# Gated linear attention's mix: from TensorE transposes to VectorE blocks sent through memory, with two roots in place of four

## The chip, the core and the metric

One core of a Trainium2 chip runs three transformer blocks as one program. The metric is device time in microseconds (us), the median of several runs. Engines by name: TensorE (PE, matmuls; PEld is its weight load), VectorE (DVE), ScalarE (ACT), GpSimd (POOL) and SyncE (SP), whose queue issues nearly all DMAs.

## The reference, cut to what matters

The change touches the end of the gated linear attention (four heads of 256 columns, 256 tokens) and the way its output reaches the product with `w_out`.

```python
    o = o_intra + o_inter.transpose(1, 2, 0, 3, 4)
    o = o.transpose(0, 2, 3, 1, 4).reshape(Bsz, S, H, DV)
    o = rms_norm(o, onorm_g)                                  # one root for each token and head
    o = o.reshape(Bsz, S, H * DV) * jax.nn.silu(r.astype(jnp.float32))
    ...
        mix = jnp.concatenate([out_a.astype(x.dtype), out_b.astype(x.dtype)], axis=-1)
        x = x + mix @ w_out[l]
```

`out_a` is this output, the first 1024 columns of the mix; `out_b` (the dilated attention) is the other half. A product contracts over the mix's columns, so they have to lie on the partitions: the mix must be transposed.

## The kernel before, in words

**The products.** Every weight matrix is streamed in units of 128 x 1024 numbers (two contraction tiles "kt" of 128 rows, 512 columns). A unit u is loaded into one of four buffers `raw` by SyncE (L2110, in order: the load of unit u + 4 is issued when VectorE is through with unit u), cut by ScalarE into a high part `wh` (L1347) and by VectorE into a low part `wl` (L1620); `wh` and `wl` have three buffers each, so the cut of unit u begins when unit u - 3 is multiplied. TensorE multiplies a unit in two halves of six matmuls (`mul`, L1154 to L1156: high by high, low by high, high by low), and the first half waits for the unit's `wl` and for the activations of its kts.

**The order of the work.** Every engine runs through one list, `plan.order`, and takes what is its own. `Plan` writes the list at build time in slots of 1.36 us (half a unit): lanes of generators say what comes when, and a `yield n` leaves n slots. What an engine finds in the list it does in that order; where it waits, all behind it on that engine waits.

**The stage around the change.** `w_out` has eight blocks of four units each (L56): first four blocks over kts 8 to 15 (the dilated half of the mix; units 101 to 116), then four over kts 0 to 7 (the gated half; units 117 to 132). While the first four run, `gla` (L534) makes the gated half: `g_o` (an output in PSUM for 128 tokens and two heads; ScalarE copies and squares it), `g_sum` (VectorE sums the squares), `g_root` (a reciprocal square root of 2 numbers per partition, 12 small VectorE instructions, L1601), `g_n` (two VectorE instructions: output times root times gate, into `va`), four times each. Then `mix` (L1166, L1357, L1632), four times, for two kts each: four TensorE transposes (L1088) into PSUM, two ScalarE instructions for the high part `mh`, two of VectorE for the low part `ml`. They stand between the halves of units 112 to 115. Unit 117 is the first to need kts 0 and 1, unit 118 kts 2 and 3, and so on.

**The way through memory**, which the kernel before uses for `x` and for nearly all mixes of the other attentions (`turned_and_sent` L416, `fetched` L430): `turn` (L1666) transposes blocks of 32 x 32 on VectorE into one of two places; `send` (L2152), four DMAs of SyncE, writes these to memory; `fetch` (L2161), one DMA, reads them back with the blocks in place; `xsent` or `msent` (L1370, L1654) cuts them into a high and a low part. Which place a turn takes alternates, and it waits until the send before the last one has landed:

```python
                    if n > 2:
                        on.wait_ge(*sent(plan.turns[n - 3]))
```

Of the kernel before, what the change touches and what calls it, by code (L numbers as in the profile page):

```python
# [152 lines left out]
class Plan:  # L153
# [276 lines left out]
    def fetched(self, p):  # L430

        yield 4
        while self.before[p] and self.before[p] not in self.said:
            yield 1
        self.say("fetch", *p)
        yield 6 if p[0] == "xsent" else 4
        self.say(*p)
# [96 lines left out]
    def gla(self):  # L534
        say = self.say
# [26 lines left out]
        for n in range(6):  # L562
            if n < 4:
                say("g_o", n)
            yield 1
            if 1 <= n < 5:
                say("g_sum", n - 1)
                say("g_root", n - 1)
            if n >= 2:
                say("g_n", n - 2)  # L570
            yield 1
        for h2 in range(2):
            for a in range(0, 4, 2):
                say("mix", "M0", 4 * h2 + a, "g", h2, a)
                yield 2

# [41 lines left out]
def program(nc, t, out):  # L618
# [76 lines left out]
    with ctx:  # L695
# [154 lines left out]
        decay = st[:, 400:416].rearrange("p (h c) -> p h c", h=4)  # L850
        rg = [st[:, 420 + 2 * m:422 + 2 * m] for m in range(4)]

        def w3(ap):
# [104 lines left out]
        def turn_places(p):  # L958

            n, (group, i) = (sents[p] - 1) % 2, plan.place[p]  # L960
            if group == "r":
                return PB[:, :, 256:384], A2[:, 5128:5640].rearrange("p (i n) -> p i n", i=4)
            first, then = {"d": (A2[:, 4096:5120], A2[:, 5120:6144]), "o": (A2[:, 2560:3584], A2[:, 3584:5632]),
                           "X1": (A2[:, 0:1024], A2[:, 4096:6144]), "X2": (A2[:, 0:1024], A2[:, 4096:6144]),
# [25 lines left out]
        def turn_place_free(p):  # L990

            kind = p[3] if p[0] == "msent" else p[1]
            if kind == "d":
                return [(s_move, moves[("move", "qk", "k", 1, 3)])]
            if kind == "X1":
                return [(s_pv, opened[("g_o", 3)]), (s_g_n, 4)]
# [41 lines left out]
        def turn_source(p):  # L1038

            if p[0] == "xsent":  # L1040
                return [x[:, k, 128 * p[2]:128 * p[2] + 256] for k in range(2)]
            return [AW[:, 512:1024] if p[3] == "o" else AW[:, 0:512]]

        def mix_source(p):

            if p[3] == "g":
                return lambda k, a: va[:, k, 512 * p[4] + 128 * (p[5] + a):512 * p[4] + 128 * (p[5] + a) + 128]
            return lambda k, a: AW[:, 512 + 256 * k + 128 * a:512 + 256 * k + 128 * a + 128]

        def turn_ready(p):  # L1050

            if p[0] == "xsent":
                return x_ready(int(p[1][1]), p[2] // 4)
            return {"d": (s_ob_dve, ob_n.get(("afin", "d", p[4]))), "r": (s_r_n, p[4] + 1), "o": (s_gated, p[4] + 1)}[p[3]]

        def gain_of(p):

            if p[0] in ("xturn", "xsent"):
                return [C(NORMS[int(p[1][1])], p[2] + i, p[2] + i + 1) for i in range(2)]
            return [C("on", 0, 1), C("on", 1, 2)] if p[3] == "g" else None  # L1060

# [20 lines left out]
        def tensor(e):  # L1082
# [8 lines left out]
            for p in plan.order:  # L1091
# [74 lines left out]
                elif kind == "mix":  # L1166
                    if p[3] == "g":
                        on.wait_ge(s_g_n, 2 * p[4] + 2)
                    else:
                        on.wait_ge(s_gated, nth("afin", "o", p[4]) - 4)  # L1170
                    on.wait_ge(*bank_free(*p))
# [412 lines left out]
        def vector(e):  # L1584
# [33 lines left out]
            for p in plan.order:  # L1618
# [307 lines left out]
                elif kind == "g_root":  # L1926
                    m = a[0]
                    root(rg[m], rg[m], 2, 256, (s_g_sum, m + 1))
                elif kind == "g_n":
                    m = a[0]  # L1930
                    k, h2 = gparts[m]
                    on.wait_ge(s_root, roots[("g_root", m)])
                    on.wait_ge(*taken(bi[("sr", 1)]))
# [330 lines left out]
```

## Time and profile before

| what | value |
|---|---|
| median of 3 runs | 1905.6 us (1905.49 to 1906.05) |
| the profiled execution, its own time | 1905.61 us |
| its span in the trace | 1903.7 us |
| TensorE busy | 1896.3 us (100%) |
| VectorE busy | 1268.9 us (67%) |
| ScalarE busy | 1001.3 us (53%) |
| DMA | 375.33 MB, mean 197 GB/s |

The span is the time from the first to the last instruction of the execution; the time beside it also has what lies around them, 1.9 us. Busy shares are over the whole span. Times inside the trace are counted from the start of the span.

### The profile page before, as it was taken

The numbers are of one execution on the slowest core, as the hardware profiler recorded it, in microseconds if no ns is written. First come the engines' busy times: TensorE is split into PE (matmuls) and PEld (weight loads), VectorE is DVE, ScalarE is ACT, GpSimd is POOL, SyncE is SP. The second block draws the span as 40 slices with busy tenths as digits, with TensorE's granted clock in tenths as the row PEclk, the third lists the DMA queues.
The fourth block names the chain that finished last, engine by engine and source line by source line (L and its number), as shares of the span: only waits on it lengthen the run. The fifth ranks groups of instructions, "written<-read, shape, count | busy, mean of one in ns | idle before, by whom it ended". The sixth has DMA issues, their size and how long they took to land.

```text
span 1903.7 us, 22784 instructions
## 1 busy us (share of the span) xinstructions
PE 1896.3 (100%) x8667; PEld 1561.9 (82%) x8667; DVE 1268.9 (67%) x1923; ACT 1001.3 (53%) x1409; POOL 14.4 (1%) x32
## 2 busy tenths in 40 slices
PE   9999999999999999999999999999999999999999
PEld 7888887888888888888888888888888888788887
DVE  6676566776666466665466776665766677777875
ACT  6777554454444344443444455654555554665653
POOL 0001000000000000000000000000000000000000
PEclk9999999999999999999999999999999999999999
DMA  9667754686666666666666786665676586555555
GB/s 323 201 189 183 208 178 133 203 256 195 195 190 196 192 188 194 196 195 197 191 194 192 219 268 194 193 194 174 195 210 195 192 263 213 165 167 165 154 169 166
DMA packets 211644, 375.33 MB, mean 197 GB/s; under 512 B 14592, under 2 KB 35376, under 8 KB 211536
## 3 DMA queue, kind: packets, MB, share of 16 engines
q1 hardware_dynamic: 210288, 371.12, 64.3%
q0 software_dynamic: 816, 2.11, 0.8%
q8 instruction: 68, 1.11, 0.2%
q10 hardware_dynamic: 432, 0.66, 0.1%
q14 instruction: 40, 0.33, 0.1%
HBM read 361.50 MB, written 12.33 MB: 196 GB/s over the span
## 4 chain that ended last, share of the span: by engine, by line
PE 98%; DVE 1%; ACT 0%; DMA 0%; issue 0%; SPq 0%; DVEq 0%; ACTq 0%
PE g L1154 31%; PE g L1156 31%; PE g L1155 31%; PE m L1223 1%; PE ob L1240 0%; PE ob L1241 0%; PE m L1088 0%; PE ob L1239 0%; DVE wl L1590 0%; PE m L1215 0%; PE m L1213 0%; DMA raw<-in_w_in 0%; PE m L1307 0%; PE ob L1294 0%; DVE st L1599 0%; PE ob L1288 0%
## 5 line engine op out<-in xcount | busy, mean ns | idle before, releaser
L1590 DVE TENSOR_TENSOR wl<-raw,wh 128x1024 fp32r<-128x1024 f32 (+1 forms) x660 | 802.6, 1217 | 559.3 <-ACT wh L1337 556.0
L1337 ACT ACTIVATE wh<-raw 128x1024 fp32r<-128x1024 f32 (+1 forms) x661 | 695.6, 1053 | 749.5 <-PE g L1156 742.1
L1154 PE MATMUL g<-wh,xh 128*128 128x512 f32 x1886 | 741.6, 393 | 0.6 <-DVE wl L1590 0.6
L1156 PE MATMUL g<-wh,xl 128*128 128x512 f32 x1886 | 735.1, 390 | 0.0
L1155 PE MATMUL g<-wl,xh 128*128 128x512 f32 x1886 | 734.5, 389 | 0.0
L1154 PEld LDWEIGHTS g<-wh,xh 128*128 128x128 f32 x1886 | 354.3, 188 | 78.7 <-issue 4.8
L1156 PEld LDWEIGHTS g<-wh,xl 128*128 128x128 f32 x1886 | 354.1, 188 | 74.4
L1155 PEld LDWEIGHTS g<-wl,xh 128*128 128x128 f32 x1886 | 354.4, 188 | 71.6
L1154 PE MATMUL g<-wh,mh 128*128 128x512 f32 x732 | 287.6, 393 | 0.0
L1156 PE MATMUL g<-wh,ml 128*128 128x512 f32 x732 | 285.2, 390 | 0.0
L1155 PE MATMUL g<-wl,mh 128*128 128x512 f32 x732 | 285.1, 390 | 0.0
L1154 PEld LDWEIGHTS g<-wh,mh 128*128 128x128 f32 x732 | 137.5, 188 | 31.6 <-issue 3.9
L1156 PEld LDWEIGHTS g<-wh,ml 128*128 128x128 f32 x732 | 137.5, 188 | 28.9
L1155 PEld LDWEIGHTS g<-wl,mh 128*128 128x128 f32 x732 | 137.5, 188 | 27.6
L1718 DVE STREAM_TRANSPOSE A<-A 32x256 f32<-32x256 f32 x176 | 76.7, 436 | 2.8
L1590 DVE TENSOR_TENSOR x<-g,x 128x512 f32<-128x512 f32 (+1 forms) x73 | 46.4, 676 | 12.1 <-PE g L1156 6.8
L1334 ACT ACTIVATE A<-g,st 128x512 f32<-128x512 f32 x50 | 31.6, 683 | 28.9 <-PE g L1156 28.9
L1337 ACT ACTIVATE A<-TW 32x256 f32<-32x256 f32 x96 | 39.9, 416 | 1.5
L1337 ACT ACTIVATE mh<-A 128x256 fp32r<-128x256 f32 (+1 forms) x56 | 26.9, 506 | 23.8 <-DVE A L1718 16.4
L1590 DVE TENSOR_TENSOR ml<-A,mh 128x256 fp32r<-128x256 f32 (+1 forms) x56 | 29.0, 540 | 13.9 <-ACT mh L1337 13.9
L1337 ACT ACTIVATE PT<-m 128x384 f32<-128x384 f32 x40 | 18.2, 489 | 37.5 <-PE m L1223 37.5
L1593 DVE SCALAR_TENSOR_TENSOR xl<-A,small,xh 128x128 fp32r<-128x128 f32 (+1 forms) x112 | 34.0, 362 | 5.4 <-ACT xh L1337 5.4
(154 smaller groups left out, 818.5 us busy)
## 6 DMA issues: line engine op xcount, KB each, us to landing
raw<-in_ev_w_in SPq DMA_DIRECT2D x128, 512.0 KB, 3.8
raw<-in_w_in SPq DMA_DIRECT2D x92, 512.0 KB, 4.3
raw<-in_w_gate SPq DMA_DIRECT2D x88, 512.0 KB, 4.4
raw<-in_w_up SPq DMA_DIRECT2D x88, 512.0 KB, 4.3
raw<-in_w_down SPq DMA_DIRECT2D x88, 512.0 KB, 4.8
raw<-in_od_w_in SPq DMA_DIRECT2D x72, 512.0 KB, 4.2
raw<-in_w_out SPq DMA_DIRECT2D x32, 512.0 KB, 4.7
raw<-in_ev_w_out SPq DMA_DIRECT2D x32, 512.0 KB, 4.8
```

Of the source, the lines that this page charges most:

```text
L1154: e.matmul(o, hi[:, kt, c], h, start=first, stop=False)
L1155: e.matmul(o, hi[:, kt, c], l, start=False, stop=False)
L1156: last = e.matmul(o, lo[:, kt, c], h, start=False, stop=end)
L1223: last = e.transpose(o[:, 128 * c:128 * c + 128], L[:, 128 * c:128 * c + 128], ident)
L1334: return e.activation(o, i, func, scale=scale, bias=bias)
L1337: return e.activation(o, i, AF.Copy, scale=scale)
L1590: return e.tensor_tensor(o, a, b, op)
L1593: return e.scalar_tensor_tensor(out=o, in0=a, scalar=s, in1=b, op0=op0, op1=op1)
L1718: last = e.transpose(dst, src)
```

## The change

The gated half of the mix takes the way through memory. `mix` for kind "g" goes; in its place stand four times `turn` (two VectorE transposes of 128 x 256 from `va`), `send`, `fetch` and `msent` (two ScalarE instructions, four of VectorE, since the norm's weight is a scale). The four roots of 2 numbers become two of 4 (one for each pair of heads), and `g_n` 0 and 1 stand behind the first, 2 and 3 behind the second.

```diff
--- before.py
+++ after.py
@@ -433,7 +433,7 @@
         while self.before[p] and self.before[p] not in self.said:
             yield 1
         self.say("fetch", *p)
-        yield 6 if p[0] == "xsent" else 4
+        yield 6 if p[0] == "xsent" or p[3] == "g" else 4
         self.say(*p)
 
     def moved_by_blocks(self, key, j):
@@ -562,17 +562,23 @@
         for n in range(6):
             if n < 4:
                 say("g_o", n)
+            else:
+                say("g_n", n - 3)
             yield 1
             if 1 <= n < 5:
                 say("g_sum", n - 1)
-                say("g_root", n - 1)
-            if n >= 2:
-                say("g_n", n - 2)
+            if n in (2, 4):
+                say("g_root", n // 2 - 1)
+            if n == 4:
+                yield from self.turned_and_sent("msent", "M0", 0, "g", 0, 0)
+            if n in (3, 5):
+                say("g_n", n - 3 if n == 3 else 3)
             yield 1
-        for h2 in range(2):
-            for a in range(0, 4, 2):
-                say("mix", "M0", 4 * h2 + a, "g", h2, a)
-                yield 2
+            if n == 4:
+                yield from self.turned_and_sent("msent", "M0", 2, "g", 0, 2)
+        for a in range(0, 4, 2):
+            yield from self.turned_and_sent("msent", "M0", 4 + a, "g", 1, a)
+            yield 1
 
     def retention(self):
         say = self.say
@@ -849,6 +855,7 @@
         nsink = st[:, 352:384]
         decay = st[:, 400:416].rearrange("p (h c) -> p h c", h=4)
         rg = [st[:, 420 + 2 * m:422 + 2 * m] for m in range(4)]
+        rg2 = [st[:, 420 + 4 * h2:424 + 4 * h2] for h2 in range(2)]
 
         def w3(ap):
             return ap.rearrange("p (t n) -> p t n", t=2)
@@ -960,7 +967,7 @@
             n, (group, i) = (sents[p] - 1) % 2, plan.place[p]
             if group == "r":
                 return PB[:, :, 256:384], A2[:, 5128:5640].rearrange("p (i n) -> p i n", i=4)
-            first, then = {"d": (A2[:, 4096:5120], A2[:, 5120:6144]), "o": (A2[:, 2560:3584], A2[:, 3584:5632]),
+            first, then = {"d": (A2[:, 4096:5120], A2[:, 5120:6144]), "g": (A2[:, 0:1024], A1[:, 1024:3072]), "o": (A2[:, 2560:3584], A2[:, 3584:5632]),
                            "X1": (A2[:, 0:1024], A2[:, 4096:6144]), "X2": (A2[:, 0:1024], A2[:, 4096:6144]),
                            "X3": (A1[:, 0:1024], A1[:, 1024:3072])}[group]
             a, b = first[:, 512 * n:512 * n + 512], then[:, 512 * i:512 * i + 512]
@@ -992,6 +999,8 @@
             kind = p[3] if p[0] == "msent" else p[1]
             if kind == "d":
                 return [(s_move, moves[("move", "qk", "k", 1, 3)])]
+            if kind == "g":
+                return [(s_pv, opened[("g_o", 3)])]
             if kind == "X1":
                 return [(s_pv, opened[("g_o", 3)]), (s_g_n, 4)]
             if kind == "r":
@@ -1039,25 +1048,26 @@
 
             if p[0] == "xsent":
                 return [x[:, k, 128 * p[2]:128 * p[2] + 256] for k in range(2)]
+            if p[3] == "g":
+                return [va[:, k, 128 * p[2]:128 * p[2] + 256] for k in range(2)]
             return [AW[:, 512:1024] if p[3] == "o" else AW[:, 0:512]]
 
         def mix_source(p):
 
-            if p[3] == "g":
-                return lambda k, a: va[:, k, 512 * p[4] + 128 * (p[5] + a):512 * p[4] + 128 * (p[5] + a) + 128]
             return lambda k, a: AW[:, 512 + 256 * k + 128 * a:512 + 256 * k + 128 * a + 128]
 
         def turn_ready(p):
 
             if p[0] == "xsent":
                 return x_ready(int(p[1][1]), p[2] // 4)
-            return {"d": (s_ob_dve, ob_n.get(("afin", "d", p[4]))), "r": (s_r_n, p[4] + 1), "o": (s_gated, p[4] + 1)}[p[3]]
+            return {"d": (s_ob_dve, ob_n.get(("afin", "d", p[4]))), "g": (s_g_n, 2 * p[4] + 2), "r": (s_r_n, p[4] + 1),
+                    "o": (s_gated, p[4] + 1)}[p[3]]
 
         def gain_of(p):
 
             if p[0] in ("xturn", "xsent"):
                 return [C(NORMS[int(p[1][1])], p[2] + i, p[2] + i + 1) for i in range(2)]
-            return [C("on", 0, 1), C("on", 1, 2)] if p[3] == "g" else None
+            return [C("on", 0, 1), C("on", 1, 2)] if p[0] == "msent" and p[3] == "g" else None
 
         def aw_free(*p):
 
@@ -1164,10 +1174,7 @@
                     four(lambda c: v[:, c // 2, 128 * (c % 2):128 * (c % 2) + 128],
                          lambda c: x[:, c % 2, 128 * (kt + c // 2):128 * (kt + c // 2) + 128]).then_inc(s_bank, 1)
                 elif kind == "mix":
-                    if p[3] == "g":
-                        on.wait_ge(s_g_n, 2 * p[4] + 2)
-                    else:
-                        on.wait_ge(s_gated, nth("afin", "o", p[4]) - 4)
+                    on.wait_ge(s_gated, nth("afin", "o", p[4]) - 4)
                     on.wait_ge(*bank_free(*p))
                     v = bank(*p)[:, :].rearrange("p (k t) -> p k t", k=2)
                     src = mix_source(p)
@@ -1924,12 +1931,12 @@
                     reduce(rg[m], (Z if m % 2 == 0 else K)[:, 512:1024].rearrange("p (g d) -> p g d", d=256),
                            ALU.add).then_inc(s_g_sum, 1)
                 elif kind == "g_root":
-                    m = a[0]
-                    root(rg[m], rg[m], 2, 256, (s_g_sum, m + 1))
+                    h2 = a[0]
+                    root(rg2[h2], rg2[h2], 4, 256, (s_g_sum, 2 * h2 + 2))
                 elif kind == "g_n":
                     m = a[0]
                     k, h2 = gparts[m]
-                    on.wait_ge(s_root, roots[("g_root", m)])
+                    on.wait_ge(s_root, roots[("g_root", h2)])
                     on.wait_ge(*taken(bi[("sr", 1)]))
                     on.wait_ge(s_pv, opened[("g_o", min(m + 2, 3))])
                     on.wait_ge(*moved("g_state", 2, h2))
```

TensorE's list loses four groups of transposes like the one here, and nothing else. Before, between the halves of unit 112:

```order
L1154 MATMUL g<-wh,mh 128x512
L1155 MATMUL g<-wl,mh 128x512
L1156 MATMUL g<-wh,ml 128x512
L1088 MATMUL m<-small,A 128x128 [waits s_g_n]
L1088 MATMUL m<-small,A 128x128 x3
L1154 MATMUL g<-wh,mh 128x512
L1155 MATMUL g<-wl,mh 128x512
```

Each group is four transposes (here the two rows of L1088); the matmuls around them stand in the same order in both lists.

VectorE's list before, from the last root on. `A<-A,st` is `g_n` 2 and 3, `wl<-raw,wh` the cuts of units 113, 114 and 115, `ml<-m` a mix, `x<-g,x` the adding of block 15:

```order
L1593 SCALAR_TENSOR_TENSOR st<-st 128x2 [waits s_dve_step]
L1593 SCALAR_TENSOR_TENSOR A<-A,st 128x256 [waits s_bank_dve,s_root]
L1593 SCALAR_TENSOR_TENSOR A<-A,st 128x256
L1590 TENSOR_TENSOR wl<-raw,wh 128x1024 [waits s_hi]
L1593 SCALAR_TENSOR_TENSOR A<-A,st 128x256 [waits s_root]
L1593 SCALAR_TENSOR_TENSOR A<-A,st 128x256
L1590 TENSOR_TENSOR wl<-raw,wh 128x1024 [waits s_hi]
L1593 SCALAR_TENSOR_TENSOR ml<-m,small,mh 128x256 [waits s_split]
L1593 SCALAR_TENSOR_TENSOR ml<-m,small,mh 128x256
L1590 TENSOR_TENSOR x<-g,x 128x512 [waits s_mul]
L1590 TENSOR_TENSOR x<-g,x 128x512
L1590 TENSOR_TENSOR wl<-raw,wh 128x1024 [waits s_hi]
```

VectorE's list of the change at the same place; the first turn and the cut of unit 113 stand just ahead of it. `A<-A 128x2x4x32` is a turn (two instructions each), `A<-A,st` is `g_n` 2 and 3, and the cuts are those of unit 114 and, first of the last row, 115:

```order
L1683 STREAM_TRANSPOSE A<-A 128x2x4x32 [waits s_send1]
L1683 STREAM_TRANSPOSE A<-A 128x2x4x32
L1600 SCALAR_TENSOR_TENSOR A<-A,st 128x256 [waits s_bank_dve,s_root]
L1600 SCALAR_TENSOR_TENSOR A<-A,st 128x256 x3
L1597 TENSOR_TENSOR wl<-raw,wh 128x1024 [waits s_hi]
L1683 STREAM_TRANSPOSE A<-A 128x2x4x32 [waits s_send0,s_g_n]
L1683 STREAM_TRANSPOSE A<-A 128x2x4x32
L1683 STREAM_TRANSPOSE A<-A 128x2x4x32 [waits s_send1]
L1683 STREAM_TRANSPOSE A<-A 128x2x4x32
L1597 TENSOR_TENSOR x<-g,x 128x512 [waits s_mul]
L1597 TENSOR_TENSOR x<-g,x 128x512
L1597 TENSOR_TENSOR wl<-raw,wh 128x1024 [waits s_hi] x3
```

The cut of unit 115 stands behind all four turns now; the third waits for the first send (`s_send0`), the fourth for the second (`s_send1`).

SyncE's list of the change. `raw<-in_w_out` is a load of weights (units 117, 118 and 119), `blocks<-A` a send (four DMAs), `A<-blocks` a fetch:

```order
L2166 DMA blocks<-A 32x4x128 [waits s_fetch0,s_turn]
L2166 DMA blocks<-A 32x4x128 x3
L1090 DMA raw<-in_w_out 128x2x512 [waits s_lo]
L2166 DMA blocks<-A 32x4x128 [waits s_fetch1,s_turn]
L2166 DMA blocks<-A 32x4x128 x3
L1090 DMA raw<-in_w_out 128x2x512 [waits s_lo]
L2166 DMA blocks<-A 32x4x128 [waits s_fetch2,s_turn]
L2166 DMA blocks<-A 32x4x128 x3
L2166 DMA blocks<-A 32x4x128 [waits s_fetch3,s_turn]
L2166 DMA blocks<-A 32x4x128 x3
L2173 DMA A<-blocks 128x512 [waits s_send0]
L1090 DMA raw<-in_w_out 128x2x512 [waits s_lo]
```

Before, nothing but loads stood here; now the first fetch is behind all four sends.

## Rows read from the trace of the kernel before

**Rows 1.** The page: busy time, granted TensorE clock in 40 slices, chain that ended last.
```profile
PE 1896.3 (100%) x8667; PEld 1561.9 (82%) x8667; DVE 1268.9 (67%) x1923; ACT 1001.3 (53%) x1409; POOL 14.4 (1%) x32
...
PEclk9999999999999999999999999999999999999999
...
PE 98%; DVE 1%; ACT 0%; DMA 0%; issue 0%; SPq 0%; DVEq 0%; ACTq 0%
```
**Rows 2.** Source line 1088 between 300 and 600 us: duration ns min/median/max, first and last start.
```profile
L1088 PE MATMUL m<-small,A x16: 270/272/273, 338.2 to 348.1; 128*128 128x128 f32 x16
```
**Rows 3.** Timeline of PE: start us, us, engine, line, operation, out<-in, count.
```profile
338.16 0.60 PE L1088 MATMUL m<-small,A 128*128 128x128 f32 x4
...
341.35 0.60 PE L1088 MATMUL m<-small,A 128*128 128x128 f32 x4
...
346.36 0.39 PE L1154 MATMUL g<-wh,mh 128*128 128x512 f32 x1
...
352.28 0.39 PE L1154 MATMUL g<-wh,mh 128*128 128x512 f32 x1
...
355.00 0.39 PE L1154 MATMUL g<-wh,mh 128*128 128x512 f32 x1
```
**Rows 4.** Timeline of DVE, 324 to 345 us; in brackets the idle time before.
```profile
324.16 0.17 DVE L1606 TENSOR_SCALAR st<-st 128x2 f32<-128x2 f32 x1
...
334.56 0.68 DVE L1599 TENSOR_REDUCE st<-A 128x2 f32<-128x512 f32 x1
335.28 0.17 DVE L1606 TENSOR_SCALAR st<-st 128x2 f32<-128x2 f32 x1
...
337.55 0.88 DVE L1593 SCALAR_TENSOR_TENSOR A<-A,st 128x256 f32<-128x256 f32 x2
338.34 1.22 DVE L1590 TENSOR_TENSOR wl<-raw,wh 128x1024 fp32r<-128x1024 f32 x1
339.48 0.88 DVE L1593 SCALAR_TENSOR_TENSOR A<-A,st 128x256 f32<-128x256 f32 x2
340.27 1.22 DVE L1590 TENSOR_TENSOR wl<-raw,wh 128x1024 fp32r<-128x1024 f32 x1
...
342.19 1.28 DVE L1590 TENSOR_TENSOR x<-g,x 128x512 f32<-128x512 f32 x2
343.38 1.22 DVE L1590 TENSOR_TENSOR wl<-raw,wh 128x1024 fp32r<-128x1024 f32 x1
```
**Rows 5.** Timeline of ACT.
```profile
331.62 1.06 ACT L1337 ACTIVATE wh<-raw 128x1024 fp32r<-128x1024 f32 x1 [0.37 <-PE g L1156]
...
377.99 0.89 ACT L1337 ACTIVATE xh<-A,small 128x256 fp32r<-128x256 f32 x2
```
**Rows 6.** Timeline of DVE, where x is turned and fetched in the same way.
```profile
365.69 0.76 DVE L1676 STREAM_TRANSPOSE A<-x 128x256 f32<-128x256 f32 x2
...
390.13 0.76 DVE L1676 STREAM_TRANSPOSE A<-x 128x256 f32<-128x256 f32 x2
390.82 1.09 DVE L1593 SCALAR_TENSOR_TENSOR xl<-A,small,xh 128x128 fp32r<-128x128 f32 x4
```
**Rows 7.** Timeline of SPq (SyncE's queue of DMA issues), 366 to 385 us.
```profile
366.49 1.83 SPq L2159 DMA_DIRECT2D blocks<-A  x4
368.48 0.39 SPq L1080 DMA_DIRECT2D raw<-in_w_out  x1
...
372.21 0.34 SPq L2166 DMA_DIRECT2D A<-blocks  x1
...
377.37 1.80 SPq L2159 DMA_DIRECT2D blocks<-A  x4
...
384.23 0.34 SPq L2166 DMA_DIRECT2D A<-blocks  x1
```
**Rows 8.** Source line 2159 (sends), 200 to 420 us: issue to landing.
```profile
DMA to landing us min/median/max: 2.1/3.5/5.5
```
**Rows 9.** Source line 2166 (fetches), the same stretch.
```profile
DMA to landing us min/median/max: 4.2/4.9/6.0
```

## The prediction

> **What bounds the kernel now.** I read the page first. TensorE is busy all the time, the chain that ended last is 98% TensorE, and its clock stands at full speed in every slice [rows 1]. So a microsecond of TensorE's list taken away is a microsecond won, and a wait of TensorE is one lost, wherever it falls. VectorE's 67% is a mean and settles nothing. I then read the stage of the gated mix from the timelines of TensorE, VectorE, ScalarE and SyncE. Between 334 and 344 us VectorE goes from one instruction to the next without idle time [rows 4]. The last question is how long a send and a fetch take; no gated mix goes that way yet, but x does 30 us later [rows 6 to 9].
>
> **What is removed.** Sixteen transposes [rows 2], in four groups. The first group begins at 338.16 and the second at 341.35, with two halves of a unit (12 matmuls in all) between them: 3.19 us. The same two halves without a group take 355.00 - 352.28 = 2.72 us [rows 3]. A group therefore costs TensorE 0.47 us, and the four cost **1.88 us**. That is all the change can win; two roots of 2.27 us (335.28 to 337.55, [rows 4]) go from VectorE too, but VectorE's time counts only where TensorE waits for it.
>
> The Trainium skill speaks against the change ("VectorE: DVE Perf Modes", The three transpose paths, and its rules for kernel authors): a full 128 x 128 transpose belongs on TensorE where a PSUM destination will do, since VectorE turns only blocks of 32 x 32. Its table gives 390 ns for one on TensorE, an estimated 6.2 us for sixteen; by that the case below in which TensorE waits for nothing would end at 1899.4 instead of 1903.7, and the sum, which ends in a wait, would stay. The row's 0.47 us for four does not agree with it, and is used.
>
> **What is added on VectorE, and where.** I build a ladder from the rows, start to start: cut of a unit 1.14 (338.34 to 339.48), `g_n` 0.79, adding a block 1.19, `g_sum` 0.72, root 2.27 [rows 4]; turn 0.69 [rows 6]. A root of 4 numbers is taken at the price of one of 2: these are tiny instructions in a dependent chain. The first root begins at 324.16 as before, and what stands ahead of the cut of unit 112 (root, block 14, cut 111, `g_sum` 2, `g_n` 0) is through at about 330.5. That cut cannot start earlier, because ScalarE's part starts at 331.62 and takes 1.06 [rows 5]. So: cut 112 at 332.7, `g_n` 1 at 333.85, `g_sum` 3 at 334.65, second root 335.35, first turn 337.6, cut 113 at 338.3, second turn 339.45, `g_n` 2 and 3 at 340.15 and 340.95, cut 114 at 341.75, and VectorE is free for the third turn at 342.9. The work saved in roots has been lost in the wait for cut 112: cut 113 stands where it stood (338.34).
>
> **The new wait.** The third turn waits until the first send has landed, the fourth until the second has, and behind them in VectorE's list stand block 15 and the cut of unit 115. A send is issued 0.80 us after its turn starts (365.69, 366.49) and takes 1.99 us of SyncE's queue (to 368.48). The first one of x was issued at 366.49, and the fetch that waits for it went at 372.21: 5.7 us [rows 6, 7]. Another took 6.9 (377.37 to 384.23). The single DMAs of sends take 2.1 to 5.5 us from issue to landing, 3.5 in the middle [rows 8], and the last of four is issued 1.4 us after the first: bounds of 3.5 and 6.9 us for a send. I take 5.7, the send that like these has one load of weights just ahead of it.
>
> The first send is then issued at 338.4 and has landed at 344.1; a load of weights follows, the second send goes at 340.9 and has landed at 346.6. Third turn 344.1, fourth 346.6, block 15 at 347.3, cut 115 at 348.5, ready (1.22 us long) at 349.7, TensorE goes on at 349.8.
>
> TensorE began unit 115 at 346.36 [rows 3]; with three groups of transposes gone it would be there at 344.95. It idles **4.85 us**. Cut 113 (ready 339.55) and cut 114 (ready 343.0) are a little late as well, 0.1 and 0.6 us; that is part of the 4.85, not on top.
>
> **The first fetch.** Unit 117 needs kts 0 and 1. From the start of unit 115 it was 352.28 - 346.36 = 5.92 us away, now 5.45: 355.25. In SyncE's list the first fetch stands behind all four sends: third send 344.9 to 346.9, fourth 347.4 to 349.4, fetch at 349.4. Fetches land after 4.2 to 6.0 us, 4.9 in the middle [rows 9]: 354.3. ScalarE's part takes 0.89 [rows 5], VectorE's 1.09 [rows 6], TensorE goes on at 356.4: **1.15 us** more. With the fetch at 4.2 it is 0.45, at 6.0 it is 2.25.
>
> After that nothing is late by this ladder. The third mix, needed by unit 119 at 361.85, is ready at 361.9. Loads of weights are issued up to 3 us later behind the sends; that of unit 119 (349.9) would be there at 354.8 if it takes as long as a fetch, and ScalarE wants it at 357. Costed at nothing: ScalarE's four pairs of instructions (as many as before), 2 MB more DMA traffic on 375 MB, VectorE's two more instructions for each mix (in time that it has while TensorE multiplies), and the later stages, whose lists are the same and which only start later. Their cover is VectorE's and ScalarE's waiting for TensorE.
>
> **Sum.** -1.88 + 4.85 + 1.15 = +4.1 us on the profiled execution's own 1905.61, which is also the median of the three runs: **1909.7 us**. The same comes out directly: unit 117 begins at 356.4 instead of 352.28, and all behind it moves with it. From no change a measurement tells about 0.2%, 3.8 us; the forecast lies just beyond.
>
> **Rivals.**
>
> *Quick sends.* For it speaks that SyncE's loads stand back here: the first send finds little else in flight, and the middle DMA of a send takes 3.5 us, so a send 4.9. Then the fourth turn starts at 345.8, cut 115 is ready at 348.9, TensorE idles 4.05, and with a fetch of 4.2 only 0.45 later on: +2.6, 1908.2 us. At the bound of 3.5 us it idles 2.65 and then 0.95, because now four sends in a row in SyncE's queue hold the fetch: +1.7, 1907.3 us. Against it speak both sends that a fetch waited for, 5.7 and 6.9. The Trainium skill ("DMA: Bandwidth & Descriptors", Anatomy of one DMA) gives a fixed 2 us, most of it the write's receipt, plus the bytes at 436 GB/s. For 64 KB that is an estimated 2.15 us, a send of 3.5 and 1907.3 us here; the rows' 3.5 us for a single DMA, under a stream of weights, do not agree with it.
>
> *Slow sends.* 6.9 us for a send and 6.0 for a fetch: TensorE goes on with unit 115 at 351.0 (6.05 idle), and waits 2.25 for the first mix: +6.4, 1912.0 us.
>
> *The clock falls.* TensorE never stops for microseconds in the trace of before, and its clock is full in all slices [rows 1]; here it stops for 4 us in one piece. If it came back at 1.2 GHz, each half of a unit (1.36 us) would take as much again: for the four halves up to unit 117 5.4 us, of which the 1.15 of waiting are hidden, 1914.0 us; for two of them 1911.2. The Trainium skill ("TensorE: Matmul & The Clock Gate", What's actually happening) says that the slow clock is the default and that an idle engine falls back to it. Nothing in the trace of before shows a fall.
>
> *Not slower.* VectorE gets the cut of unit 115 ready before TensorE wants it, at 344.9, and the 1.88 us stand alone: 1903.7 us. It decides whether that cut starts by 343.65. Even without any wait for a landing the ladder has it at 342.9 + two turns + block 15 = 345.45 and ready at 346.65, so VectorE would have to be 1.8 us faster than its rows, and the first fetch as much earlier.
>
> **How the numbers follow.** Forecast 0.50 (its own range 1908.9 to 1910.8), quick sends 0.27, slow sends 0.13, clock 0.05, not slower 0.05. Slower by over 0.2% (above 1909.4): some two thirds of the forecast's case, the slow sends and the clock: 0.52. Within 0.2%: the rest of the forecast, the quick sends and nearly all of the last case (-1.9 us is within it as well): 0.46. Faster: 0.02. The range goes from 1907.0 (just under the quick sends' bound) to 1912.6 (just over the slow ones).
>
> **What would show it.** No L1088 transposes into mh's banks between 338 and 348 us; VectorE's turns start at about 337.6, 339.5, 344.1 and 346.6, the last two with idle time ahead that a DMA into memory ended; TensorE idle for some 4 us before unit 115, released by the low part of the weights, and about 1 us before unit 117, released by the low part of the mix. TensorE's other rows are unchanged. The prediction is wrong if the fourth turn starts before 344, if TensorE idles elsewhere (a load of weights late behind the sends), or if the clock's row shows less than 9.

## The result, and the profile after

The change takes **1908.65 us** (median of 20 runs, 1907.59 to 1909.64); the kernel before, on the same chip, 1905.45 (20 runs, 1905.24 to 1906.08). The ratio is 1.0016, with a 95% interval of 1.001 to 1.0022: 3.2 us slower. The profiled execution of the change took 1909.28 us (span 1907.5), against 1905.61 (span 1903.7) before: 3.67 us more.

The page of the change, where [rows 1] stood: busy time, granted TensorE clock in 40 slices, and the chain that ended last.

```profile
PE 1897.8 (99%) x8651; PEld 1561.1 (82%) x8651; DVE 1268.9 (67%) x1915; ACT 1001.0 (52%) x1409; POOL 14.4 (1%) x32
...
PEclk9999999999999999999999999999999999999999
...
PE 97%; DVE 2%; ACT 0%; SPq 0%; DMA 0%; issue 0%; DVEq 0%; ACTq 0%
```

TensorE has 16 instructions less, as the diff says, and yet 1.5 us more of busy time: some of the rest became slower. The chain now goes through VectorE for 2% of the span, where 1% stood (both are rounded). The clock's row shows nothing; its slices are 48 us long.

The list of waits of the change (engine and line that waited, what for: us in total, times, longest) has one wait of TensorE for a low part of the weights that is longer than 2 us, and one turn that waited for a send:

```profile
PE g L1164 <- DVE wl L1597: 2.9, 2, 2.5
...
DVE A L1683 <- DMA blocks<-A: 1.8, 1, 1.8
```

VectorE's timeline of the change (start, duration, then engine, line, operation, out<-in, count; in brackets the idle time before and what ended it), against [rows 4]:

```profile
332.85 1.23 DVE L1597 TENSOR_TENSOR wl<-raw,wh 128x1024 fp32r<-128x1024 f32 x1 [2.32 <-ACT wh L1344]
...
337.76 0.77 DVE L1683 STREAM_TRANSPOSE A<-A 128x256 f32<-128x256 f32 x2
338.45 1.18 DVE L1597 TENSOR_TENSOR wl<-raw,wh 128x1024 fp32r<-128x1024 f32 x1
...
341.79 1.22 DVE L1597 TENSOR_TENSOR wl<-raw,wh 128x1024 fp32r<-128x1024 f32 x1
342.93 0.77 DVE L1683 STREAM_TRANSPOSE A<-A 128x256 f32<-128x256 f32 x2
345.49 0.77 DVE L1683 STREAM_TRANSPOSE A<-A 128x256 f32<-128x256 f32 x2 [1.79 <-DMA blocks<-A]
346.18 1.25 DVE L1597 TENSOR_TENSOR x<-g,x 128x512 f32<-128x512 f32 x2
347.36 3.47 DVE L1597 TENSOR_TENSOR wl<-raw,wh 128x1024 fp32r<-128x1024 f32 x3
```

The cut of unit 112 (332.85) still waits for ScalarE, so the shorter roots bring nothing; from there to the cut of unit 114 the predicted ladder holds to within 0.2 us. Then comes the fourth turn, which waits 1.79 us for the second send. The third turn did not wait. Behind the fourth stand block 15 and the cut of unit 115 (347.36, before 343.38).

TensorE's timeline of the change, against [rows 3]:

```profile
345.69 0.39 PE L1166 MATMUL g<-wh,ml 128*128 128x512 f32 x1
348.61 0.53 PE L1164 MATMUL g<-wh,mh 128*128 128x512 f32 x1 [2.54 <-DVE wl L1597]
348.95 0.62 PE L1165 MATMUL g<-wl,mh 128*128 128x512 f32 x1
...
351.93 0.60 PE L1166 MATMUL g<-wh,ml 128*128 128x512 f32 x1
352.36 0.41 PE L1164 MATMUL g<-wh,mh 128*128 128x512 f32 x1
...
355.80 0.39 PE L1164 MATMUL g<-wh,mh 128*128 128x512 f32 x1
```

The last matmul of unit 114 starts at 345.69 and unit 115 begins at 348.61. After that stop the matmuls do not come every 0.23 us but every 0.42, up to 352.36. Unit 117 (355.80) finds its activations ready; nothing holds it. The table by stretch (busy time and instructions of each engine, then the granted clock, the DMA share and GB/s) shows what the 40 slices hide:

```profile
340.00:349.00 9.00, 6.11 (x26) 4.39 (x25) 7.21 (x14) 3.10 (x3) 0.00 (x0) 1.00 0.82 222
349.00:352.50 3.50, 3.50 (x10) 2.73 (x9) 2.45 (x5) 0.91 (x2) 0.00 (x0) 0.52 0.91 233
352.50:360.00 7.50, 7.50 (x35) 6.18 (x34) 6.10 (x15) 5.60 (x9) 0.00 (x0) 1.00 0.87 314
```

The granted clock was 0.52 for 3.5 us, that is, nearly all of it at the lower level of 1.2 GHz, after a stop of 2.54 us. It did not fall during the stop: read in shorter stretches it is 1.00 from 345.5 to 348.6 and 0.50 only from 349.0 on, when TensorE has been at work again for 0.4 us. Of the 20 runs 12 have a mean clock of 0.999 and a median of 1908.8 us; the other 8 have 1.000 and a median of 1907.88. So the fall comes in some runs and not in others, with the same program. The mean clock is a coarse sign of it: it has three digits, and a fall to half for under some 1.9 us (an estimate: half of that is 0.0005 of 1907 us) would still read 1.000. Five of the 8 took 1907.6 to 1908.0 us, the other three 1908.3 to 1908.6, and those may hide a short one.

SyncE's queue in the change, against [rows 7]; `blocks<-A` is a send, `A<-blocks` a fetch:

```profile
338.56 1.78 SPq L2166 DMA_DIRECT2D blocks<-A  x4
340.38 0.45 SPq L1090 DMA_DIRECT2D raw<-in_w_out  x1
340.93 1.88 SPq L2166 DMA_DIRECT2D blocks<-A  x4
...
343.72 4.29 SPq L2166 DMA_DIRECT2D blocks<-A  x8
348.06 0.44 SPq L2173 DMA_DIRECT2D A<-blocks  x1
```

The trace's answers from issue to landing (minimum, median, maximum), against [rows 8, 9]: the first send, the second send, and the four fetches of the change.

```profile
DMA to landing us min/median/max: 1.7/1.8/1.8
...
DMA to landing us min/median/max: 3.0/3.1/3.3
...
DMA to landing us min/median/max: 2.8/5.7/6.4
```

The second send, issued at 340.93, had landed when the fourth turn began at 345.49: 4.56 us. The first was issued at 338.56 and cannot have taken more than 4.37, since the third turn began at 342.93 without a wait; its last DMA was issued at 339.9 and none took more than 1.8, so it took about 3.1. The first fetch landed in 2.8 us: ScalarE began its mix at 350.87, the low part was ready at 353.0, and TensorE came to it only at 355.80.

**The sum as measured.** All earlier work of this trace lies 0.14 us later than before (the cut of unit 112 by ScalarE begins at 331.76 instead of 331.62). Without three groups of transposes unit 115 would begin at 346.36 - 1.41 + 0.14 = 345.09; it begins at 348.61: 3.52. From there to unit 117 it is 7.19 us instead of 5.45: 1.74, nearly all of it for the clock. (Some 0.14 of it is the start after a stop: in the last kernel below, after a stop of 0.74 us and with a clock of 1.00, two halves of a unit take 2.86 us instead of 2.72.) So -1.88 + 3.52 + 1.74 = +3.38, and with the 0.14 the 3.52 by which unit 117 is later than before, of 3.67 in all.

### The profile page after: what moved, and what is told of

It is laid out like the page before. It is cut to its first block, busy times and chain, and to the rows that moved or that the text cites. A ratio compares the mean times of both kernels' runs of the same rounds, so it can differ in the third digit from the quotient of the medians.

```text
span 1907.5 us, 22773 instructions
## 1 busy us (share of the span) xinstructions
PE 1897.8 (99%) x8651; PEld 1561.1 (82%) x8651; DVE 1268.9 (67%) x1915; ACT 1001.0 (52%) x1409; POOL 14.4 (1%) x32
## 4 chain that ended last, share of the span: by engine, by line
PE 97%; DVE 2%; ACT 0%; SPq 0%; DMA 0%; issue 0%; DVEq 0%; ACTq 0%
PE g L1164 31%; PE g L1166 31%; PE g L1165 31%; PE m L1230 1%; DVE wl L1597 0%; PE ob L1247 0%; PE ob L1248 0%; PE ob L1246 0%; PE m L1098 0%; PE m L1222 0%; PE m L1220 0%; PE m L1314 0%; DVE st L1606 0%; PE ob L1301 0%; PE ob L1295 0%; PE m L1106 0%
```

## The experiments

Eight kernels were run, each 11 times beside the kernel before on the same chip. What is called "the theory" in the expectations is: the transposes are worth 1.9 us, the staging places make VectorE late for the cut of unit 115, and the clock falls after that stop.

### What the transposes cost: twice as many

The kernel before, with the sixteen transposes made twice:

```diff
-                    four(lambda c: v[:, c // 2, 128 * (c % 2):128 * (c % 2) + 128],
-                         lambda c: src(c % 2, c // 2)).then_inc(s_bank, 1)
+                    for i in range(2 if p[3] == "g" else 1):
+                        last = four(lambda c: v[:, c // 2, 128 * (c % 2):128 * (c % 2) + 128],
+                                    lambda c: src(c % 2, c // 2))
+                    last.then_inc(s_bank, 1)
```

> The kernel before, with each of the sixteen transposes of the gated mix made twice by TensorE into the same place. It measures by itself what the change takes away. Theory (0.47 us for a group, of which some 0.12 is the switch between shapes, which is not doubled): 4 x 0.35 to 0.47 = 1.4 to 1.9 us more than before, 1906.9 to 1907.4. Rival (a transpose costs what it lasts, 0.27 us, or the weights' way is the limit): 16 x 0.27 = 4.3 us, 1909.8.

It took 1907.46 us (1907.24 to 1908.47), the kernel before 1905.55; ratio 1.0011, interval 1.0002 to 1.002. TensorE's timeline of this kernel:

```profile
338.11 1.03 PE L1088 MATMUL m<-small,A 128*128 128x128 f32 x8
...
341.74 1.03 PE L1088 MATMUL m<-small,A 128*128 128x128 f32 x8
```

From group to group it is 3.63 us, with groups of four 3.19 [rows 3]. A doubled group costs 0.44 more, four of them 1.76, and the median rose by 1.9. The interval is wide for so small a difference, but all 11 runs lie above all 33 of the kernel before (1905.19 to 1906.03). That agrees with the 1.88 us, and with TensorE's list being paid for one to one here.

The Trainium skill ("VectorE: DVE Perf Modes", The three transpose paths) gives 390 ns for a 128 x 128 transpose on TensorE, in a table for bf16, while these are fp32; by that the doubling would have cost an estimated 6.2 us. The runs do not agree: one more transpose in a row costs 0.11 us.

### The wait for the staging place: a place for each turn

The change, with a place of their own for the third and fourth turn and four semaphores for the sends, so that no turn has to wait for a landing:

```diff
+            if group == "g" and i >= 2:
+                first = A1[:, 5120:6144]
...
-            return s_send[n % 2], 64 * (n // 2 + 1)
+            return s_send[n % 4], 64 * (n // 4 + 1)
...
-                    if n > 2:
+                    if n > 2 and not (a[0] == "msent" and a[3] == "g" and plan.place[a][1] >= 2):
                         on.wait_ge(*sent(plan.turns[n - 3]))
```

> The third and fourth turn of the change get staging places and send semaphores of their own, so that no turn waits for a landing; the order of every engine stays. Theory (the fourth turn's wait for the second send, 1.79 us, is what makes the cut of unit 115 late, and the stop it makes is long enough to bring the slow clock): fourth turn at 343.6 right behind the third, cut 115 at about 345.6, TensorE goes on at about 346.9 instead of 348.6, idle about 1.8 us before unit 115; no fall of the clock, so 1907.6 - 1.75 = 1905.9 us in every run, beside 1905.45 of before. First rival (the landings cost nothing; VectorE's work or the loads of weights are late by themselves): 1907.6 to 1908.7 as the change. Second rival (the first fetch behind four sends takes over): TensorE waits before unit 117 for up to 1 us, 1906.9.

It took 1907.7 us (1907.13 to 1908.19), beside 1905.55; ratio 1.0011, interval 1.0003 to 1.002. That was missed: about 1 us better than the change, and 1.8 us worse than expected. Even this 1 us can be the clock alone: the change's own runs with a mean clock of 1.000 have a median of 1907.88. VectorE's timeline shows that the edit does what it should:

```profile
342.68 1.42 DVE L1685 STREAM_TRANSPOSE A<-A 128x256 f32<-128x256 f32 x4
...
345.19 2.34 DVE L1599 TENSOR_TENSOR wl<-raw,wh 128x1024 fp32r<-128x1024 f32 x2
```

Four transposes stand in a row with no idle time, and the cut of unit 115 begins at 345.19 instead of 347.36. TensorE's timeline shows where the gain went, at the starts of units 115, 117, 118 and 119:

```profile
346.45 0.50 PE L1166 MATMUL g<-wh,mh 128*128 128x512 f32 x1 [0.62 <-DVE wl L1599]
...
352.84 0.47 PE L1166 MATMUL g<-wh,mh 128*128 128x512 f32 x1 [0.65 <-issue]
...
356.23 0.47 PE L1166 MATMUL g<-wh,mh 128*128 128x512 f32 x1 [0.38 <-DVE ml L1602]
...
359.61 0.47 PE L1166 MATMUL g<-wh,mh 128*128 128x512 f32 x1 [0.40 <-DVE ml L1602]
```

From unit 115 to 117 it is 6.39 us instead of 5.45, and then twice some 3.38 instead of 2.72: 2.27 us of waiting for the mixes. Unit 119 begins 1.89 us later than before (357.72 there), and the whole execution was 1.93 longer. The fetches are the cause. This is the answer of the trace for the four of them:

```profile
DMA to landing us min/median/max: 3.3/6.2/6.8
```

They are issued from 347.27 on, less than 1 us earlier than in the change, because all four sends still stand ahead of them in SyncE's list. ScalarE waits for the first one, and VectorE for ScalarE, in their timelines:

```profile
350.58 0.91 ACT L1346 ACTIVATE mh<-A,small 128x256 fp32r<-128x256 f32 x2 [3.60 <-DMA A<-blocks]
...
351.60 1.14 DVE L1602 SCALAR_TENSOR_TENSOR ml<-A,small,mh 128x128 fp32r<-128x128 f32 x4 [2.93 <-ACT mh L1346]
```

The low part is through at 352.74 and unit 117 begins at 352.84, though the record of that matmul calls its wait "issue". TensorE arrives 2.2 us earlier than in the change and finds nothing ready. So two chains end nearly together here: the staging place's, and send, issue queue and fetch. To take away the first uncovers the second, as the second rival of the expectation had it, but for three units and not for one. No stop between 322 and 372 us is longer than 0.65 us by the records, and the mean clock is 1.000 in all runs.

### The fall of the clock: fill the stop

The change, with fourteen matmuls that nobody reads, ahead of unit 115:

```diff
+                    if u == 115 and half == 0:
+                        for i in range(14):
+                            e.matmul(MB[0][:, :], mh[:, 8, 0:128], mh[:, 8:10, :], start=True, stop=True)
```

> The change, with 14 matmuls more on TensorE just before unit 115 into a PSUM bank that nobody reads, so that TensorE works through most of the time in which it waits for the cut of unit 115 (14 x 0.23 = 3.2 us of 3.5). Theory (the stop lets the clock fall, and this is what splits the 20 runs of the change into 1907.6 to 1908.0 with a mean clock of 1.000 and around 1908.7 with 0.999): all runs at a mean clock of 1.000 and 1907.6 to 1907.9 us, 1 us less than the change's median although TensorE does more, and matmul starts 0.23 us apart after unit 115 begins. Rival (the 1 us comes from transfers that land later in some runs, and the clock only goes with it): two groups of runs as before, median 1908.7.

It took 1907.57 us (1907.32 to 1909.05), beside 1905.55; ratio 1.0012, interval 1.0003 to 1.0021. TensorE's timeline of this kernel:

```profile
345.59 3.34 PE L1143 MATMUL m<-mh 128*128 128x512 f32 x14
348.77 0.39 PE L1167 MATMUL g<-wh,mh 128*128 128x512 f32 x1
349.00 0.40 PE L1168 MATMUL g<-wl,mh 128*128 128x512 f32 x1
...
360.28 0.47 PE L1167 MATMUL g<-wh,mh 128*128 128x512 f32 x1 [0.40 <-DVE ml L1603]
```

The row of its table by stretch that answers to the slow one of the change:

```profile
349.00:352.50 3.50, 3.50 (x17) 2.90 (x16) 2.41 (x5) 1.61 (x3) 0.00 (x0) 1.00 0.88 227
```

TensorE is as late for unit 115 as in the change (348.77), but it was at work, and the clock stays at 1.00: matmuls every 0.23 us, 17 of them in a stretch in which the change got 10 done. The fall is therefore a consequence of the stop, and more work makes the kernel 1.1 us faster (1908.65 for the change, and 1908.7 for its twin of the next experiment, which ran beside this one on the same chip). It is less than the 1.74 us that the clock took in the trace: at full clock TensorE comes to unit 119 before its mix, and waits 0.55 us from start to start (359.50 + 0.23 to 360.28). Slow matmuls had covered that. Eight of the 11 runs took 1907.3 to 1907.7, three 1908.2 to 1909.05, all with a mean clock of 1.000. A varying lateness of the fetches would fit, but only one of these executions (1908.18) has a trace, so what sets the three apart stays open.

### The number of roots, in the change

The change with four roots of 2 numbers, as before (the planner is also told that a root costs half, so that the order of the rest stays):

```diff
-            if n in (2, 4):
-                say("g_root", n // 2 - 1)
+                say("g_root", n - 1)
...
-                    h2 = a[0]
-                    root(rg2[h2], rg2[h2], 4, 256, (s_g_sum, 2 * h2 + 2))
+                    m = a[0]
+                    root(rg[m], rg[m], 2, 256, (s_g_sum, m + 1))
```

> The change with four roots of 2 numbers again, one behind each sum, and the planner told that they cost half, so that all else stands nearly where the change has it (two turns of x one unit earlier). Theory (two roots in place of four won nothing, because VectorE waits 2.32 us before the cut of unit 112 in the change and has room for one of them, and the other stands where the joint root stood): cut 113 at 338.3 to 338.5, the time equal to the change, 1907.6 or 1908.7 as the clock goes. Rival (each root on VectorE's path counts 2.27 us): turns 2 to 4.5 us later, TensorE waits as much longer before unit 115, 1910.5 to 1912.

It took 1908.7 us (1907.9 to 1909.09), beside 1905.55; ratio 1.0016, interval 1.0007 to 1.0025. That is the time of the change. VectorE's timeline of this kernel:

```profile
338.31 1.18 DVE L1596 TENSOR_TENSOR wl<-raw,wh 128x1024 fp32r<-128x1024 f32 x1
...
345.31 0.77 DVE L1682 STREAM_TRANSPOSE A<-A 128x256 f32<-128x256 f32 x2 [1.76 <-DMA blocks<-A]
```

TensorE's:

```profile
348.44 0.50 PE L1163 MATMUL g<-wh,mh 128*128 128x512 f32 x1 [2.51 <-DVE wl L1596]
```

The cut of unit 113, the wait and the stop are those of the change, to 0.2 us. The two roots saved fall into the 2.32 us in which VectorE waits for ScalarE's part of unit 112.

### The two roots alone

The kernel before with two roots of 4 numbers, and the mix on TensorE as it was:

```diff
-                say("g_root", n - 1)
-            if n >= 2:
-                say("g_n", n - 2)
+            if n in (2, 4):
+                say("g_root", n // 2 - 1)
+            if n >= 3:
+                say("g_n", n - 3)
+            if n == 5:
+                say("g_n", 3)
```

> The kernel before with two roots of 4 numbers in place of four, the mix still turned by TensorE: the half of the change that leaves TensorE's list alone. Theory (TensorE waits for nothing in this stage before, so VectorE's saved time wins nothing): 1905.5 us, no difference, VectorE idle some 2.3 us more before the cut of unit 112. Rival (the shorter chain lets the mix and all behind it come earlier): 1903 to 1905.

It took 1905.37 us (1905.14 to 1906.22), beside 1905.6; ratio 0.9999, interval 0.999 to 1.0008. Nothing, as expected. In VectorE's timeline of this kernel

```profile
337.43 1.22 DVE L1593 TENSOR_TENSOR wl<-raw,wh 128x1024 fp32r<-128x1024 f32 x1
```

is the cut of unit 113, 0.9 us earlier than in [rows 4], and TensorE does not ask for it earlier.

### The third and fourth turn behind the cuts

The change, with block 15 and the cut of unit 115 ahead of the third turn, and the cut of unit 116 ahead of the fourth:

```diff
+        yield 2
         for a in range(0, 4, 2):
             yield from self.turned_and_sent("msent", "M0", 4 + a, "g", 1, a)
-            yield 1
+            yield 2
```

> The change with its third turn behind block 15 and the cut of unit 115, and its fourth behind the cut of unit 116: the order alone, with two staging places as in the change. Theory (the stop before unit 115 is a matter of what stands behind the waiting turn): TensorE goes on with unit 115 without a stop of more than 0.2 us, the clock never falls; but the third and fourth mix come 3 us later than in the change, and TensorE waits before unit 119 for 1.4 to 3 us: 1906 to 1907.5. Rival (the time goes to the transfers whatever the order): 1907.6 or more.

It took 1908.84 us (1907.23 to 1910.1), beside 1905.6; ratio 1.0015, interval 1.0006 to 1.0024. Missed: that is in the range of the rival. There is no stop ahead of unit 115 any more, but TensorE's timeline shows such a stop 11 us later, ahead of unit 119:

```profile
359.74 0.47 PE L1165 MATMUL g<-wh,mh 128*128 128x512 f32 x1 [2.63 <-DVE ml L1601]
...
361.36 0.63 PE L1167 MATMUL g<-wh,ml 128*128 128x512 f32 x1
```

SyncE's timeline has the third fetch,

```profile
351.30 0.52 SPq L2174 DMA_DIRECT2D A<-blocks  x1
```

and ScalarE's the instructions that wait for it:

```profile
357.45 0.91 ACT L1345 ACTIVATE mh<-A,small 128x256 fp32r<-128x256 f32 x2 [2.33 <-DMA A<-blocks]
```

It is issued at 351.30 and has landed by 357.45, 6.15 us later; TensorE stopped for 2.63 us, and the clock fell again (0.63 us a matmul, in 6 of the 11 runs by their mean clock). The turns can be early, and delay a cut, or late, and delay a mix.

### The turns in VectorE's idle time

The change, with `g_n` 0 and 1 and the first two turns ahead of the cut of unit 112, where VectorE has been waiting for ScalarE in every kernel so far:

```diff
-            if n == 4:
+            if n == 3:
+                say("g_n", 0)
+                say("g_n", 1)
                 yield from self.turned_and_sent("msent", "M0", 0, "g", 0, 0)
...
+                yield from self.turned_and_sent("msent", "M0", 2, "g", 0, 2)
             yield 1
...
+            if n >= 4:
+                say("g_n", n - 2)
```

> The change with another order: g_n 0 and 1 and the first two turns and sends stand ahead of the cut of unit 112, in the 2.32 us in which VectorE waited for ScalarE; the second root, g_n 2 and 3 and the last two turns move up behind them. Theory (the way through memory is worth its 1.88 us once no turn finds a send under way and the first fetch isn't behind four sends): first turn at about 331.1, first fetch at about 338.6, third and fourth turn at 340.7 and 341.4 without a wait, cut 115 at 343.3, TensorE never stops between 325 and 360 us, 1905.5 - 1.9 = 1903.6 to 1903.7 us, faster than both kernels. Rival (as the run with places of its own showed, when one stop goes the next limit comes up: the fetches of kts 4 to 7 are issued with loads of weights and land after 6 us): TensorE waits before unit 119, 0.4 us or more, 1904.0 to 1904.6. Second rival (loads of weights are late behind early sends): stops at units 116 or 117, 1905 or more.

It took **1903.72 us** (1903.45 to 1904.54), beside 1905.6; ratio 0.999, interval 0.9981 to 0.9999. It beats both kernels: the kernel before by 1.88 us, what the transposes cost. The interval nearly reaches 1, but all 11 runs lie below all 33 of the kernel before (1905.34 to 1906.45). VectorE's timeline:

```profile
331.20 1.42 DVE L1682 STREAM_TRANSPOSE A<-A 128x256 f32<-128x256 f32 x4
332.69 1.23 DVE L1596 TENSOR_TENSOR wl<-raw,wh 128x1024 fp32r<-128x1024 f32 x1
...
340.79 1.43 DVE L1682 STREAM_TRANSPOSE A<-A 128x256 f32<-128x256 f32 x4
...
343.31 2.34 DVE L1596 TENSOR_TENSOR wl<-raw,wh 128x1024 fp32r<-128x1024 f32 x2
```

The third and fourth turn come 9 us after the first two, when the places are long free, and the cut of unit 115 begins at 343.31, just before the 343.65 that the rival "not slower" asked for. The first two fetches go at 338.50, nearly ten us before those of the change, so that the 4.3 to 7.0 us that fetches take here are hidden. TensorE has no idle time between 330 and 370 us.

### The same with four roots

The order of the kernel just above with four roots of 2 numbers (its edit and that of "The number of roots, in the change" together).

> The early order with four roots of 2 numbers in place of two of 4, all else of the plan the same. Theory (in this order VectorE has no wait left that would hide a root, so the two roots count): cut 113 late by 0.5 us and cut 115 at about 345.3, 2 us later than with two roots; TensorE stops about 0.7 and 1.0 us, 1903.65 + 1.7 = 1905.3 us. Rival (the roots don't matter in any order, as in the change): the time of the early order.

It took 1905.64 us (1905.3 to 1906.07), beside 1905.6; ratio 1.0, interval 0.9991 to 1.0009. Now TensorE stops twice for the low part of the weights, as its timeline shows:

```profile
340.43 0.50 PE L1162 MATMUL g<-wh,mh 128*128 128x512 f32 x1 [0.73 <-DVE wl L1595]
...
346.91 0.50 PE L1162 MATMUL g<-wh,mh 128*128 128x512 f32 x1 [0.74 <-DVE wl L1595]
```

In this order VectorE has nothing left over, and the two roots saved are worth 1.9 us. (The unit after this second stop begins at 349.77; the granted clock is 1.00 there.) The same edit was worth nothing in the kernel before and nothing in the change.

## Why the prediction was right, point by point

The forecast was 1909.7 us and the measurement 1908.65: 4.1 us slower forecast, 3.2 found. The direction, the place and the wait were right; two terms of the sum were too large, and one that stood among the rivals took part of their room. The time lies below the forecast's own narrow range (from 1908.9) and within the 0.2% for which the prediction had the smaller chance (0.46, against 0.52 for more).

1. **Transposes, -1.88.** Right: 0.44 for each doubled group, 1.9 us in the median.
2. **Roots are worth nothing.** Right, shown twice, by four roots in the change and by two roots alone.
3. **The ladder up to the cut of unit 114.** Right to 0.2 us: first turn 337.76 (337.6), cut of unit 113 338.45 (338.3), cut of unit 114 341.79 (341.75).
4. **Idle time ahead of unit 115, 4.85.** Right in kind, too large: 3.52, of which 2.54 is one stop; most of the rest was lost at unit 114, as the ladder had it. The term that was mis-sized is the 5.7 us for a send. It came from a send of x with other traffic about. Here the first send took about 3.1, below the lower bound of 3.5, and the second 4.56, so the third turn waited for nothing and the fourth began at 345.49 instead of 346.6. The rival "quick sends" (4.9 us a send, idle 4.05, 1908.2 us) was nearer to this than the forecast, in the wait and in the time.
5. **First fetch, 1.15.** Wrong in the change: TensorE did not wait for it at all. The fetch was issued at 348.06, 1.3 us earlier than in the ladder, and it landed in 2.8 us, below all of [rows 9]. The mix was through at 353.02, so that TensorE would not have waited without the slow matmuls either (355.80 less 1.74). But the fetches are the next to be late: they cost 2.27 us as soon as the first wait is taken away, and 0.55 in the trace where the stop is filled.
6. **The clock.** This had a chance of 0.05, and it came in 12 of 20 runs. The price was also too high: two or four halves at half speed were reckoned, and it was one and a third, some 1.6 us in the trace (1.74 with the start after the stop) and 1.1 between the medians of the change and of the kernel with the stop filled. The Trainium skill ("TensorE: Matmul & The Clock Gate", What's actually happening) says that an idle engine falls back to the lower clock; the trace agrees, 0.52 after the stop and 1.00 where the stop was filled. To hold "no fall is seen in the trace of before" against it was weak: once TensorE is under way, no wait of it in that trace is longer than 1.1 us. And the sign that the prediction named, a clock row below 9, could not show it: the row reads 9 throughout, and the clock fell.

The sum of the forecast (-1.88 + 4.85 + 1.15 = +4.1) and that of the trace (-1.88 + 3.52 + 1.74 = +3.4) are near each other in part by luck: the stop and the fetch came out 2.5 us smaller than forecast (1.33 and 1.15), and the clock, which the sum had at nothing, put 1.74 back. Without the clock the change would have taken 1907.9 by its own eight runs with a mean clock of 1.000, and 1907.6 by the kernel with the stop filled; the forecast was 1.8 to 2.1 us above that.

## What to carry to other kernels

Taking work off the engine that sets the time pays only as long as what replaces it finds idle time on the others, so put it where an engine waits anyway: the same turns cost 3.2 us behind the cut of unit 112 and won 1.9 us ahead of it. With two chains that end nearly together (a staging place that must be free, a fetch behind four sends in one queue), take one away and the other shows; give both their lead at once, by issuing earlier. Cost a stop of some 2.5 us by its idle time plus, in part of the runs, a stretch at half clock, and read the clock in a table of short stretches, since slices of 48 us hide it.

## What the runs showed of the hardware that was not expected

- **One stop, then half speed.** After TensorE stood for 2.54 us in the middle of a program that had run at full clock, the granted clock was 0.52 for 3.5 us. It began to fall only after the engine was back at work: in the change 0.3 to 0.4 us after, with late turns 0.8 us (restart at 359.74 after 2.63 us, first slow matmul at 360.52). By the mean clock of each run it came in 12 of 20 runs of the change, 9 of 11 with four roots and 6 of 11 with late turns. Stops of 0.4 to 0.7 us were followed by no fall. What decides between two runs of the same program was not found.
- **Filler work can win.** Fourteen useless matmuls in the stop made the program 1.1 us faster.
- **Landing times went with their company.** In the change a DMA of the first send landed in 1.8 us, one of the second, with a load of weights just ahead in SyncE's queue, in 3.1; of four fetches the first, right behind the sends, took 2.8 us, and the others, issued after one or two more loads, 5.3, 6.2 and 6.4. No run changes the company alone, so this cause is not shown. The Trainium skill ("DMA: Bandwidth & Descriptors", Anatomy of one DMA) gives, for DMAs that GpSimd issues, a fixed 2 us plus the bytes, an estimated 2.15 us for one DMA of a send (64 KB). The prediction's rival used that figure without saying so, and these DMAs are SyncE's. The first send is near it (1.8), the second is not.
